# Ten modulation-weight products of the attention loop on GpSimd instead of VectorE

## The reference, cut to what matters

```python
c_silu = jax.nn.silu(c)                                  # 1 x 1024
mods = jnp.split(c_silu @ ada_w[layer] + ada_b[layer], N_MOD, axis=-1)   # 9 vectors of 1024 a layer
sh, sc, g = mods[0], mods[1], mods[2]
h = modulate(rms_norm_2(x, norm_g[layer, 0]), sh, sc)
...
shift, scale = jnp.split(c_silu @ kv_ada_w + kv_ada_b, 2, axis=-1)
```

## Time and profile before

| | us |
|---|---|
| median of 3 runs | 1420.74 |
| lowest, highest | 1418.81, 1422.39 |
| the profiled execution's own time | 1418.81 |
| its span in the profile | 1417.0 |

### The profile page before, as it was taken

The page is one execution under the profiler, slowest core; times in us unless marked ns, Lnnn a source line. Parts: engine busy times, 40 slices in busy tenths (PEclk is TensorE's granted clock), DMA queues, the critical chain, the costliest instruction groups (busy, mean ns, idle before and its releaser), DMA issues.

```text
span 1417.0 us, 16660 instructions
## 1 busy us (share of the span) xinstructions
PE 1354.1 (96%) x6759; PEld 1113.5 (79%) x6759; DVE 935.5 (66%) x1063; ACT 658.3 (46%) x861; POOL 24.6 (2%) x48
## 2 busy tenths in 40 slices
PE   7999788999999999998999999999999998999998
PEld 6986457788887788887788888878888886788887
DVE  4456977766567866667866667676666757754444
ACT  4444664644446533434534435553334555633442
POOL 2200000000000000000000000000000000000000
PEclk9989899999999999999999999999999999999999
DMA  9878656687878578785577884567787531365551
GB/s 248 228 233 226 227 190 220 240 291 263 296 262 291 188 261 292 280 280 171 188 272 272 281 304 147 170 243 258 254 284 282 192 119 60 114 213 179 187 197 61
DMA packets 165568, 317.55 MB, mean 224 GB/s; under 512 B 7018, under 2 KB 114852, under 8 KB 156276
## 3 DMA queue, kind: packets, MB, share of 16 engines
q1 hardware_dynamic: 161872, 305.50, 63.1%
q0 software_dynamic: 3440, 10.93, 2.8%
q10 hardware_dynamic: 180, 0.05, 0.0%
HBM read 314.10 MB, written 1.84 MB: 223 GB/s over the span
## 4 chain that ended last, share of the span: by engine, by line
PE 86%; DVE 9%; ACT 2%; issue 2%; DMA 1%; ACTq 0%; DVEq 0%
PE bank L696 26%; PE bank L698 26%; PE bank L697 26%; PE bank L793 2%; DVE full L1770 1%; DVE wlo L1703 1%; PE bank L716 1%; PE bank L743 1%; PE bank L719 1%; DMA ada<-in_ada_w 1%; DVE acc L1690 1%; DVE xt L1758 1%; DVE mix L1756 1%; ACT whi L1309 1%; DVE ulo L1783 0%
## 5 line engine op out<-in xcount | busy, mean ns | idle before, releaser
L1703 DVE TENSOR_TENSOR wlo<-raw,whi 128x2048 fp32r<-128x2048 f32 x205 | 469.3, 2291 | 270.0 <-ACT whi L1309 269.7
L1309 ACT ACTIVATE whi<-raw 128x2048 fp32r<-128x2048 f32 x205 | 392.1, 1913 | 199.9 <-PE bank L698 194.2
L696 PE MATMUL bank<-whi,uhi 128*128 128x512 f32 (+2 forms) x1088 | 430.1, 395 | 12.2 <-DVE ulo L1783 4.7
L698 PE MATMUL bank<-whi,ulo 128*128 128x512 f32 (+2 forms) x1088 | 420.1, 386 | 0.0
L697 PE MATMUL bank<-wlo,uhi 128*128 128x512 f32 (+2 forms) x1088 | 419.2, 385 | 0.0
L696 PEld LDWEIGHTS bank<-whi,uhi 128*128 128x128 f32 x1088 | 206.8, 190 | 58.2 <-issue 16.9
L698 PEld LDWEIGHTS bank<-whi,ulo 128*128 128x128 f32 x1088 | 206.4, 190 | 42.1
L697 PEld LDWEIGHTS bank<-wlo,uhi 128*128 128x128 f32 x1088 | 207.0, 190 | 39.6 <-issue 1.2
L696 PE MATMUL bank<-whi,hsplit 128*128 128x512 f32 (+1 forms) x512 | 202.5, 395 | 2.1 <-DVE hsplit L1847 2.1
L698 PE MATMUL bank<-whi,hsplit 128*128 128x512 f32 (+1 forms) x512 | 199.9, 391 | 0.0
L697 PE MATMUL bank<-wlo,hsplit 128*128 128x512 f32 (+1 forms) x512 | 199.7, 390 | 0.0
(11 more groups left out here) (254 smaller groups left out, 1050.0 us busy)
## 6 DMA issues: line engine op xcount, KB each, us to landing
raw<-in_ffn_w_in SPq DMA_DIRECT2D x176, 512.0 KB, 4.8
ada<-in_ada_w SPq DMA_DIRECT2D x72, 1024.0 KB, 7.4
raw<-in_ffn_w_out SPq DMA_DIRECT2D x44, 1024.0 KB, 5.1
raw<-in_w_in SPq DMA_DIRECT2D x16, 1024.0 KB, 7.4
raw<-in_w_mlp_in SPq DMA_DIRECT2D x16, 1024.0 KB, 6.2
raw<-in_w_mlp_out SPq DMA_DIRECT2D x16, 1024.0 KB, 5.1
ada<-in_kv_ada_w SPq DMA_DIRECT2D x8, 1024.0 KB, 7.7
raw<-in_w_kv SPq DMA_DIRECT2D x8, 1024.0 KB, 5.3
```

What stands on the lines that cost most here:

```text
L696: nc.tensor.matmul(o, sh, mh, start=start, stop=False, skip_group_check=skip)
L698: return nc.tensor.matmul(o, sl, mh, start=False, stop=stop, skip_group_check=skip)
L1309: ins = nc.scalar.activation(whi[:, ring(n), :], raw[:, ring(n), :], ACT.Copy)
L1703: ins = nc.vector.tensor_tensor(wlo[:, ring(n), :], raw[:, ring(n), :], whi[:, ring(n), :].bitcast(F32), ALU.subtract)
```

## The change

The call of `job` leaves VectorE's loop of pairs, and the same ten jobs are written into GpSimd's block, behind the bias tables and ahead of the wait for the end of the loop. GpSimd has two instructions for each job but job 8: it scales `ada` in place, waits for its own scaling, and adds it to the accumulator. Job 8, the first of its pair, is one scaling; it waits for `cs_prob` since `acc[:, 1]` holds other data until then. SyncE's block and the jobs outside the loop are as before.

```diff
+        ada_scaled = sem("ada_scaled")
...
+            scaled = [0]
+            for j in PAIR_JOBS.values():
+                pair, k = j // KT, j % KT
+                a = acc[:, pair % 2, :]
+                pool.wait_ge(ada_loaded[j % 2], 16 * (j // 2 + 1))
+                pool.wait_ge(ada_used, j)
+                if k == 0:
+                    pool.wait_ge(cs_prob, 1)
+                    nc.gpsimd.tensor_scalar(a, ada[:, j % 2, :], csilu[:, 0:1], None, ALU.mult).then_inc(ada_used, 1)
+                else:
+                    ada_j = ada[:, j % 2, :]
+                    nc.gpsimd.tensor_scalar(ada_j, ada_j, csilu[:, k:k + 1], None, ALU.mult).then_inc(ada_scaled, 1)
+                    scaled[0] += 1
+                    pool.wait_ge(ada_scaled, scaled[0])
+                    nc.gpsimd.tensor_tensor(a, a, ada_j, ALU.add).then_inc(ada_used, 1)
+
             pool.wait_ge(s_max, NU)
...
                 if i in PAIR_CONV:
                     conv(PAIR_CONV[i])
-                if i in PAIR_JOBS:
-                    job(PAIR_JOBS[i])
             for q in range(2):
```

## The result

| | before | with the change |
|---|---|---|
| median, us | 1421.31 (4 runs) | 1489.12 (4 runs) |
| lowest to highest, us | 1418.81 to 1422.39 | 1487.77 to 1491.16 |
| the profiled execution, us | 1418.81 | 1491.16 |

The ratio is 1.0481, with an interval of 1.0462 to 1.05: the change makes the kernel 68 us slower. The prediction said slower, by 36 us, with 1470 as its upper end; the time lies 19 us above that end.

What follows compares the result with a forecast made beforehand. VectorE was taken to bound the loop of pairs; GpSimd's 69 us, VectorE's 48.5 and 8 idle, less 11 overlapped, made 114.5 us, +36 over 79. Forecast 1456 us, range 1408 to 1470.

Steps and rivals of the forecast that it cites:

- What bounds the kernel: Loop of pairs, 129 to 208 us: VectorE, busy 70.9 of 79 us, sets the pace; TensorE is full only from 174 to 193.
- What is removed: In the loop, the ten jobs' 22.4 us leave VectorE, which keeps 48.5 us of work.
- the rival: No exclusion: GpSimd's work in the loop costs VectorE nothing, so 10 us faster, 1411 us; chance 0.25.
- What GpSimd's instructions take: In the loop, a scaling takes 2.5 us and an addition 4.9; ten scalings and nine additions make 69 us.
- the prediction's own sum: Loop time as GpSimd's 69 us, VectorE's 48.5 and 8 idle, less 11 overlapped: 114.5 us, +36 over 79.
- Whether the work is free beside VectorE: In the loop, GpSimd's instructions and VectorE's wide readers exclude each other through a shared memory path: +36 us, chance 0.60.
- The size of the overlap: VectorE gets 0.6 us ahead during each of GpSimd's 19 instructions in the loop, 11 us together.
- The idle time kept at 8.1: VectorE keeps its 8.1 us of idle time in the loop unchanged.
- the sentence that a slower loop adds nothing by its clock: A slower loop leaves TensorE at the 1.2 GHz level more often; nothing added, since TensorE is not the bound then.
- The queues: GpSimd's loads and jobs alternate, ending near 220 us before the loop's end near 244; SyncE's later `w_out` loads stay hidden.
- The range: Whole kernel: 1408 to 1470 us, meant to hold 8 in 10, reaching into the faster case.
- the likeliest case: Exclusion in the loop as summed: 1438 to 1470 us, from floor +19 to ceiling +46.5 with 3 for the clock; chance 0.60.

Runs made afterwards that it cites:

- experiment 5: Changed kernel with all ten jobs on one column and `acc[:, 1]` cleared once ahead of the loop, other columns' products left out: 1415.39 us, ratio 0.995.
- experiment 2: Changed kernel with GpSimd's nineteen scalings and additions replaced by clearings of the same 128x2048 tiles, the products' values left out: 1428.86 us, ratio 1.0043.
- Experiment 3: Changed kernel with the loads of jobs 6 and 7 put ahead of the third `w_up` slot in SyncE's queue: 1487.46 us, ratio 1.0464.
- experiment 7: Two variants of the changed kernel: first, only VectorE's double-rate scalings in single-rate forms, 1460.09 us; second, only its small two-input instructions replaced, 1491.13 us.
- experiment 1: Changed kernel with each GpSimd job but job 8 on one of its 2048 columns, waits and loads kept: 1419.60 us, ratio 0.998.
- experiment 4: Changed kernel with VectorE's small loop instructions rewritten so none reads two SBUF tiles or runs at double rate, everything computed: 1432.44 us, ratio 1.0071.

## Why the prediction was wrong in size

**What bounds the kernel** held in the direction that mattered. VectorE sets the pace of the loop when it is made to stand: it stood for some 82 us, and the kernel takes 73.7 us longer than in experiment 5, where nothing holds it. In the other direction it held only for a few microseconds: with 22.4 us of work taken off, the loop became 5.8 us shorter and then waited for the hand-overs.

**What is removed** held: the products' 22.4 us are gone. What that is worth by itself was too high in the rival, 10 us where experiment 5 has 5.8. (The products' rows overlap their neighbours': by experiment 5 the rest of VectorE's work fills 50.3 us and not 48.5.)

**What GpSimd's instructions take** is the step that failed. The scaling was put at 2.5 us, with the clearing's slope as the bound from above. It took 5.44. The clearing was no bound for it: a clearing of 2048 columns takes 1.80 us (experiment 2), so a scaling costs GpSimd three times as much. The addition was put at 4.9 and took 4.5. Together they are 96.1 us and not 69. With 96.1 the prediction's own sum gives a loop of 96.1 + 48.5 + 8 - 11 = 141.6 us, 63 more than before: 1483 where 1489 was measured. The Trainium skill (GPSIMD Engine Reference, section on elementwise cycle accounting) gives 4.50 us for the addition; the trace agrees, with 4.49 to 4.56.

**Whether the work is free beside VectorE** held as the mechanism, which the chances had at 0.60 and no row could show. L1927, with two SBUF inputs, stands 4.49 us beside an addition and has 0.16 beside a clearing, and the scaling with a written sum keeps its 475 ns. The Trainium skill (SBUF — State Buffer, section "Who interferes with whom") says that a VectorE instruction with two SBUF inputs contends with a GpSimd one that reads SBUF and not with one that only writes, and that the form of `tensor_scalar` that writes its accumulator stays out of the shared ports; the traces agree with both. The size of the overlap held roughly too. The account of the loop, in us, with VectorE's work without the products at 48.5 in both:

| | before | forecast | measured |
|---|---|---|---|
| VectorE's work | 48.5 + 22.4 | 48.5 | 48.5 |
| standing in a hold | 0 | 69 - 11 = 58 | 131.1 - 48.5 = 82.6 |
| idle | 8.1 | 8.1 | 147.7 - 131.1 = 16.6 |
| the loop | 79 | 114.6 | 147.7 |

(131.1 is VectorE's busy time in the window 129 to 276.7 of the changed kernel.) GpSimd ran for 96.1 us and VectorE stood for 82.6 of them, so it got 13.5 us ahead, where 11 was said; with the 50.3 us of experiment 5 as its work these are 80.8 and 15.3, so both are good to some 2 us. Of the missing 33 us, 24.6 are the longer standing: GpSimd's 27.1 us more, of which the scalings are +30.4 and the additions -3.3, less the 2.5 us that VectorE got further ahead.

**The idle time kept at 8.1** is the other 8.5 us, and was a choice: "8.1 us of idle time" was carried over as if it were fixed. Behind GpSimd's last hold at 248.5 us VectorE waited 4.21 us for TensorE's bank:

```profile
256.97 0.29 DVE L1922 CUSTOM_DVE_ANT_0 mix<-bank,acc 128x128 f32<-128x128 f32 x1 [4.21 <-PE bank L1054]
```

The windows of that moment (columns as above) show that TensorE was then full or nearly so:

```profile
249.00:257.00 8.00, 7.84 (x42) 5.34 (x43) 3.23 (x20) 4.64 (x11) 0.00 (x0) 0.79 0.00 0
257.00:266.00 9.00, 7.28 (x51) 4.61 (x49) 8.54 (x39) 5.30 (x21) 0.00 (x0) 1.00 0.26 79
```

These are iterations 9 and 10, in which TensorE multiplies gate weights, and before too it was full there: 19.00 of 19.00 us from 174 to 193, at a granted clock of 1.00. Now the first 8 us have a granted clock of 0.79 of the 2.4 GHz level; here the sentence that a slower loop adds nothing by its clock was wrong in its reason, since TensorE is the bound for these 8 us. The clock is not all of it. In experiment 5, with no hold at all and a clock of 0.91 in the loop, VectorE is idle for 24 of 74 us: once the products are gone, it waits for TensorE and for hand-overs wherever it does not stand. So idle time had to grow with the products gone, and 8.1 was too low for that reason alone. How much of the 8.5 us is the clock and how much is this no run separates.

**The queues** held in their result and not in their course. SyncE's issues:

```profile
181.32 0.61 SPq L564 DMA_DIRECT2D raw<-in_w_up_swa  x1
...
182.63 1.08 SPq L534 DMA_DIRECT2D ada<-in_ada_w  x2
...
262.55 0.38 SPq L518 DMA_DIRECT2D raw<-in_w_out  x1
```

The third `w_up` slot was issued at 181.32, where the kernel before has it at 152.57, and GpSimd's 20-us gap follows from it; I had loads and jobs alternate to about 220, and GpSimd ended at 248.5. `w_out` was issued at 262.55, 14 us ahead of the loop's end, as it was before (194.30 and 208). Experiment 3 moved the gap and the time stayed; it did not remove it.

**The range** was too narrow on the side that the likeliest case had. Its top of +46.5 counted every term at its ceiling but took the ceiling of the scaling from another kind of instruction.

## What to carry to other kernels

Work moved to GpSimd is not free beside a busy VectorE, even when GpSimd was idle for the whole stretch: here each microsecond of GpSimd's scalings and additions cost about 0.77 us of the loop, although the instructions of VectorE that stood take 0.16 to 0.35 us by themselves, since a hold catches the next one that shares a path. Before such a move, look in every stage of the chain on VectorE for one scaling at double rate or one instruction with two SBUF inputs; by experiment 7 one left in a stage is enough for the stop, and to remove only its neighbour, as the second of the two kernels did, wins nothing. In the trace, read the longest row of a small instruction, not its mean: 0.17 us as the median and 5.0 us as the longest is a stop, not a load.

## What the runs showed of the hardware beyond that

- On GpSimd the scaling by a column of scalars, with one tile to read, is slower than the addition of two tiles: 5.44 against 4.50 us for 128x2048 f32, and a clearing takes 1.80. On one column the scaling and the addition take 0.28 and 0.19 us (experiment 1).
- The exclusion goes both ways: a scaling of GpSimd was stretched from 5.44 to 7.59 us by one of VectorE's conversions in experiment 4.
- A clearing stops VectorE's double-rate scalings only (up to 1.92 us in experiment 2); an instruction that reads stops its two-input ones as well (4.49 us in the changed kernel).
- A scaling that also writes its sum passes beside GpSimd, at 346 and 475 ns where the plain one has 286 and 348 alone (128 and 256 columns).

Not tried: the ten products at other places of VectorE's order, or their sum as matmuls. No kernel that computes everything beat the one before.
